# Two transformer layers on one core: the factor of the norm ahead of the gate product moved to the gate's output, norm weights multiplied ahead, the mixer's last tiles released one by one, the tail in halves

## The reference, cut to what matters

```python
mix = nsa_gmlp_mixer(rms_norm_2(h, norm_mix_pre), ...)      # ends in mixed @ w_out
h = h + rms_norm_2(mix, norm_mix_post)
gate, up = split(rms_norm_2(h, norm_ffn_pre) @ w_gate_up)   # 2816 columns each
ffn = (silu(gate) * up) @ w_down
h = h + rms_norm_2(ffn, norm_ffn_post)
# rms_norm_2(x, g) = x * rsqrt(mean(x * x) + 1e-6) * g
```

## Time and profile before

| | |
|---|---|
| runs | 1069.22, 1070.29, 1072.54 us (median 1070.29) |
| profiled execution | 1068.46 us |
| its span, first to last instruction | 1066.7 us |
| PE busy | 997.9 us (94%) |
| DVE, ACT, POOL busy | 407.6, 388.4, 391.0 us (36 to 38%) |
| mean granted PE clock | 0.985 of full |
| moved by DMA | 92.81 MB, mean 87 GB/s |

### The profile page before, as it was taken

How to read it: one execution, slowest core, us unless ns; L and a number is a source line. 1 busy time by engine, 2 the same in 40 slices (tenths; PEclk the granted TensorE clock), 3 DMA queues, 4 the chain that set the end, 5 groups by cost and what they waited for, 6 DMA issues and landing times.

```text
span 1066.7 us, 13142 instructions
## 1 busy us (share of the span) xinstructions
PE 997.9 (94%) x5055; PEld 816.8 (77%) x5055; DVE 407.6 (38%) x906; ACT 388.4 (36%) x720; POOL 391.0 (37%) x314
## 2 busy tenths in 40 slices
PE   6979999999998999989989899599999999999995
PEld 3867777767877887978878788488888888888884
DVE  3462631349655344437468642630000000122224
ACT  4232332343835233243555544432222322233332
POOL 4461422234221524123320015535444444454443
PEclk9989999999999999999999999799999999999998
DMA  6752121122115331052230002142323323232311
GB/s 225 201 176 48 48 72 40 42 78 65 40 41 198 119 119 61 23 181 77 75 104 2 1 1 82 41 136 79 104 94 91 106 81 117 80 119 79 119 40 79
DMA packets 68062, 92.81 MB, mean 87 GB/s; under 512 B 9740, under 2 KB 47153, under 8 KB 68000
## 3 DMA queue, kind: packets, MB, share of 16 engines
q1 hardware_dynamic: 68000, 91.97, 26.7%
HBM read 89.82 MB, written 6.85 MB: 91 GB/s over the span
## 4 chain that ended last, share of the span: by engine, by line
PE 82%; DVE 10%; issue 3%; ACT 2%; POOL 2%; DMA 1%; SPq 0%; DVEq 0%; ACTq 0%
PE psum L1010 62%; PE psum L1251 5%; PE psum L1211 4%; PE psum L1226 2%; POOL st L2099 1%; PE psum L1303 1%; PE psum L1084 1%; DVE prob L1837 1%; PE psum L1179 1%; PE psum L1279 1%; DVE sq L1739 1%; PE psum L1264 1%; DVE R L1867 1%; PE psum L1047 1%; PE psum L1293 1%
## 5 line engine op out<-in xcount | busy, mean ns | idle before, releaser
L2071 POOL TENSOR_TENSOR WR<-RAW,WR 128x512 fp32r<-128x512 f32 (+2 forms) x268 | 341.4, 1282 | 578.7 <-ACT WR L1390 578.7
L1010 PE MATMUL psum<-WR,XT 128*128 128x512 f32 (+2 forms) x2160 | 500.9, 387 | 5.8 <-DVE st L747 2.6
L1010 PEld LDWEIGHTS psum<-WR,XT 128*128 128x128 f32 x2160 | 390.3, 190 | 81.6 <-DVE st L747 3.4
L1390 ACT ACTIVATE WR<-RAW 128x512 fp32r<-128x512 f32 (+2 forms) x268 | 161.3, 615 | 263.3 <-PE psum L1010 251.0
L1010 PE MATMUL psum<-XT,WR 128*128 128x512 f32 x1056 | 241.8, 391 | 1.5 <-issue 1.5
L1010 PEld LDWEIGHTS psum<-XT,WR 128*128 128x128 f32 x1056 | 198.9, 189 | 43.1 <-issue 1.8
L1518 ACT ACTIVATE prob<-prob,st 128x512 f32<-128x512 f32 (+2 forms) x112 | 58.9, 547 | 160.4 <-DVE st L1837 146.7
L1692 DVE TENSOR_TENSOR actT<-psum,gated 128x512 f32<-128x512 f32 x22 | 14.2, 686 | 203.3 <-ACT gated L1470 203.3
L1251 PE MATMUL psum<-ones_up,probT 128*128 128x128 f32 x536 | 77.2, 285 | 12.5 <-DVE R L1867 8.3
L1251 PEld LDWEIGHTS psum<-ones_up,probT 128*128 128x128 f32 x536 | 68.5, 196 | 21.1 <-issue 13.7
L2028 DVE TENSOR_TENSOR XT<-actT,XT 128x512 fp32r<-128x512 f32 x22 | 28.4, 1290 | 84.6 <-ACT XT L1575 84.6
(11 more groups left out here) (210 smaller groups left out, 753.2 us busy)
## 6 DMA issues: line engine op xcount, KB each, us to landing
RAW<-in_w_gate_up_dram SPq DMA_DIRECT2D x44, 512.0 KB, 4.5
RAW<-in_w_in_dram SPq DMA_DIRECT2D x16, 1024.0 KB, 5.3
RAW<-in_w_down_dram SPq DMA_DIRECT2D x11, 1024.0 KB, 4.9
RAW<-in_w_out_dram SPq DMA_DIRECT2D x8, 1024.0 KB, 5.1
RAW<-in_w_in_dram SPq DMA_DIRECT2D x12, 512.0 KB, 4.5
rep_scratch<-rows_scratch SPq DMA_DIRECT2D x12, 320.0 KB, 7.2
R<-in_x_dram SPq DMA_DIRECT2D x4, 512.0 KB, 5.6
x_again<-in_x_dram SPq DMA_DIRECT2D x1, 2048.0 KB, 7.8
```

The costliest lines, as they stand in the source:

```text
L1010: last = pe.matmul(outp, stationary(x), moving(y), start=start and n == 0, stop=stop and n == 2)
L1390: act.activation(WR[:, s % RING, 0, 0:w], RAW[:, g % 2, q, 0:w], ACT.Copy).then_inc(w_hi, 1)
L2071: pool.tensor_tensor(WR[:, s % RING, 1, 0:w], RAW[:, g % 2, q, 0:w], WR[:, s % RING, 0, 0:w].bitcast(F32), ALU.subtract).then_inc(w_lo, 1)
```

## The change

- **The factor r1 and the weights.** With y the mixer's product, h = x + r1·y·g1. The new kernel does not form h before the gate product. During `out2` chunk 0 DVE makes XG = x·g0 (`xg`) and GG = g0·g1 (`gains`); `sqa` and `yg` make YG = y·g0·g1; `gx` makes YG·r1 + XG = h·g0 in one instruction per half, which is transposed.
- **The factor r2** of the norm ahead of the gate product is left out of the product's input. h itself (`res`, two DVE instructions of 128x1024 per tile) and its squares (`sq gu`) are made during gate chunk 0; r2 (`rr_x`) is then written to DRAM as a row of 512 values and read back broadcast to all partitions (`r_bc`, SP, `spread_r`). Every gate output is multiplied by it on DVE ahead of silu; the up output is not, and since the norm at the end takes out a factor of each token, only its epsilon is changed (`eps_x`).
- **Tiles released one by one.** The last k-step of `out2` is split into steps by tile (`mq`), with transposes of `xt gu` between them; the second half of y is copied out of its bank by ACT (`ycopy`), and the gate product waits for that (`y_copied`). The splits of gate slots 0 to 2 move from `out2` into this stretch.
- **Chunk 0 is evacuated later**, after k-step 3 of chunk 1.
- **The tail by halves.** Each tile's last down products go half by half; squares, the product with the gain (`yf`), the residual and the store (256 KB) are done for each half, all on DVE; POOL keeps the power.

The diff, cut to its core:

```diff
@@ make_timeline, out_product
-                if (phase, c, n) == ("out2", 1, KD - 1):
-                    tl.append(("mm", phase, c, n))
+                if (phase, c) == ("out2", 1) and n >= 4:
+                    tl.extend([("mm", phase, c, n)] if n < KD - 1 else [])
                 elif c or n >= begun:
                     mm(phase, c, n)
+                if phase == "out2" and c == 0 and n >= 4:
+                    tl.append(("xg", n - 4))
...
             if phase == "out2" and c == 0:
+                tl.append(("gains",))
                 tl.extend(("sqa", t) for t in range(NT))
@@ make_timeline, behind out2
-    for steps in (mix[0], post[0], mix[1], post[1], sq_gu[0], mix[2], post[2], sq_gu[1], mix[3], post[3], gx_gu[0][:1], gx_gu[1][:1], sq_gu[2]):
-        tl.extend(steps)
...
+    def finish(t):
+        return [("sq", "mix", t), ("ms", "mix", t), ("yg", t)]
+    row = [("mm", "out2", 1, KD - 1)] + [("mq", "out2", 1, KD - 1, t) for t in range(1, NT)]
+    tl.extend([row[0]] + finish(0))
+    tl.extend([row[1], ("gx", "gu", 0, 0)] + finish(1))
+    tl.extend([row[2], ("gx", "gu", 1, 0)] + finish(2) + [("xt", "gu", 0, 0), ("ycopy", 0)])
+    tl.extend([row[3], ("gx", "gu", 2, 0)] + finish(3) + [("gx", "gu", 3, 0), ("xt", "gu", 1, 0), ("xt", "gu", 2, 0)])
+    tl.extend([("split", first["gu", 0]), ("ycopy", 1), ("xt", "gu", 3, 0), ("ycopy", 2), ("ycopy", 3)])
+    tl.extend(("split", first["gu", 0] + j) for j in (1, 2))
+    tl.append(("split", first["gu", 0] + 3))
+    tl.append(("gx", "gu", 0, 1))
...
+            if c == 0 and 2 < k < 7:
+                tl.extend([("res", k - 3), ("sq", "gu", k - 3)])
+            if c == 0 and k == 6:
+                tl.append(("ms", "gu"))
+            if c == 1 and k == 3:
+                tl.append(("ev", "gu", 0))
+        if c:
+            tl.append(("ev", "gu", c))
...
+    for t in range(NT):
+        tl.extend([("sq", "ffn", t), ("yf", t, 0), ("ms", "ffn", t), ("yf", t, 1), ("post", "ffn", t)])
@@ SP
+            def spread_r():
+                sp.wait_ge(r_ready, nth["ms", "gu"] + 1)
+                sp.wait_ge(gx_done, nth["gx", "gu", 3, 1] + 1)
+                    sp.dma_start(r_d.rearrange("o (t p) -> p (o t)", p=P), rr_x).then_inc(r_stored, 16)
+                sp.wait_ge(r_stored, 16)
+                sp.dma_start(r_bc[:, :], r_d.broadcast_to([P, SEQ])).then_inc(rbc_done, 16)
...
-                index["gu", 2, 0]: [lambda: load_gain(1, "norm_ffn_post_2", (post_dve, NT))],
+                index["gu", 2, 0]: [spread_r, lambda: load_gain(1, "norm_ffn_post_2", (res_done, NT))],
...
+                for hf in range(2):
+                    cols = slice(512 * hf, 512 * hf + 512)
+                    sp.wait_ge(post_dve, 2 * t + hf + 1)
+                    sp.dma_start(out_v[:, t, cols], R2[:, t, cols]).then_inc(s_out, 16)
@@ PE
-                            order = [(kt, hf, t) for t in range(NT) for kt in tiles for hf in range(2)]
+                            order = [(kt, hf, t) for t in range(NT) for hf in range(2) for kt in tiles]
...
-                            pe.wait_ge(post_dve, NT)
+                            pe.wait_ge(y_copied, NT)
@@ ACT
+                elif what == "ycopy":
+                    act.wait_ge(yg_done, t + 1)
+                    act.activation(R1[:, t, 512:D], MM[t], ACT.Copy).then_inc(y_copied, 1)
...
-                            act.activation(gated[:, m, :], SET[ch % 2][m], ACT.Silu).then_inc(gs_done, 1)
+                            act.wait_ge(gate_scaled, 2 * ch + m + 1)
+                            act.activation(gated[:, m, :], gated[:, m, :], ACT.Silu).then_inc(gs_done, 1)
@@ DVE
+                        ins = dve.scalar_tensor_tensor(out=YG[:, t, cols], in0=YG[:, t, cols], scalar=rr[:, t:t + 1],
+                                                       in1=XG[:, t, cols], op0=ALU.mult, op1=ALU.add)
...
+                        dve.scalar_tensor_tensor(out=ss[:, t:t + 1], in0=ss[:, t:t + 1], scalar=floor, in1=ss_a[:, t:t + 1],
+                                                 op0=ALU.add, op1=ALU.add).then_inc(ms_ready, 1)
...
+                    dve.tensor_tensor(XG[:, t, :], R2[:, t, :], gain[0][:, :], ALU.mult).then_inc(xg_done, 1)
+                    dve.tensor_tensor(GG[:, :], gain[0][:, :], gain[1][:, :], ALU.mult).then_inc(gains_done, 1)
+                    dve.tensor_tensor(YG[:, t, 512:D], MM[t], GG[:, 512:D], ALU.mult).then_inc(yg_done, 1)
...
+                elif what == "res":
+                    dve.wait_ge(y_copied, t + 1)
+                    link(dve.tensor_tensor(R1[:, t, :], R1[:, t, :], gain[1][:, :], ALU.mult))
+                    dve.scalar_tensor_tensor(out=R2[:, t, :], in0=R1[:, t, :], scalar=rr[:, t:t + 1], in1=R2[:, t, :],
+                                             op0=ALU.mult, op1=ALU.add).then_inc(res_done, 1)
...
+                    last = dve.tensor_tensor(R1[:, t, cols], SET[hf][t], gain[1][:, cols], ALU.mult)
...
+                        dve.wait_ge(w_used, first[phase, ch] + KD)
+                        if ch == 0:
+                            dve.wait_ge(rbc_done, 16)
+                        for m in range(2):
+                            dve.tensor_tensor(gated[:, m, :], SET[ch % 2][m], r_bc[:, :], ALU.mult).then_inc(gate_scaled, 1)
...
+                    for hf in range(2):
+                        cols = slice(512 * hf, 512 * hf + 512)
+                        dve.scalar_tensor_tensor(out=R2[:, t, cols], in0=R1[:, t, cols], scalar=rr[:, t:t + 1], in1=R2[:, t, cols],
+                                                 op0=ALU.mult, op1=ALU.add).then_inc(post_dve, 1)
@@ POOL
-                if what == "post":
-                    pool.tensor_tensor(R2[:, t, cols], R2[:, t, cols], R1[:, t, cols], ALU.add).then_inc(post_pool, 1)
```

More of the change, by code:

```diff
@@ L575, in hybrid_two_block_kernel @@
         hot_r = sem("cmp_hots_copied")
+        gains_done = sem("gains_multiplied")
+        yga_done = sem("first_half_times_gains")
+        yg_done = sem("second_half_times_gains")
+        y_copied = sem("second_half_copied")
+        xg_done = sem("rows_times_pre_gain")
+        res_done = sem("residual_done")
+        r_stored = sem("r_row_stored")
+        rbc_done = sem("r_row_landed")
+        gate_scaled = sem("ffn_gate_scaled")
+        ffn_sq = sem("ffn_squares_summed")
         post_dve = sem("post_by_dve")
-        post_scaled = sem("post_scaled")
-        post_pool = sem("post_by_pool")
         xt_in = sem("xt_transposed")
@@ L961, in load_gmlp @@
                 bcast(ln_b[:, :], a["gmlp_ln_b_2"], 512).then_inc(s_gm_in, 16)
+            def spread_r():
+                sp.wait_ge(r_ready, nth["ms", "gu"] + 1)
+                sp.wait_ge(gx_done, nth["gx", "gu", 3, 1] + 1)
+                with nc.allow_non_contiguous_dma(reason="one row of 512 words, once"):
+                    sp.dma_start(r_d.rearrange("o (t p) -> p (o t)", p=P), rr_x).then_inc(r_stored, 16)
+                sp.wait_ge(r_stored, 16)
+                sp.dma_start(r_bc[:, :], r_d.broadcast_to([P, SEQ])).then_inc(rbc_done, 16)
             def load_gain(n, name, pre):
@@ L1085, in _ @@
                     last.then_inc(xt_in, 1)
-                elif what == "mm":
-                    _, phase, ch, n = step
+                elif what in ("mm", "mq"):
+                    _, phase, ch, n = step[:4]
                     s = first[phase, ch] + n
@@ L1116, in _ @@
                                     last.then_inc(w_used, 1)
[L1117 removed]
+                            elif kt == ch:
                                 last.then_inc(down_rows, 1)
@@ L1123, in _ @@
                     k = k_tile(phase, n)
-                    pe.wait_ge(w_lo, s + 1)
-                    if ch == 0 and n % 4 == 0:
+                    tiles = range(NT)
+                    if what == "mq":
+                        tiles = [step[4]]
+                    elif ("mq", phase, ch, n, 1) in nth:
+                        tiles = [0]
+                    if what == "mm":
+                        pe.wait_ge(w_lo, s + 1)
+                    if ch == 0 and n % 4 == 0 and what == "mm":
                         wait_rows(pe, phase, 1 if phase == "in1" else halves(phase)[n // 4], xt_lo)
@@ L1135, in _ @@
                     prev = ("ev", phase, ch - 1) if ch else {"in2": ("ev", "out1", 1)}.get(phase)
-                    for t in range(NT):
+                    for t in tiles:
                         if n == 0 and prev and phase != "gu":
@@ L1156, in _ @@
                                 last.then_inc(bank_full, 1)
-                    last.then_inc(w_used, 1)
+                    if NT - 1 in tiles:
+                        last.then_inc(w_used, 1)
                 elif what == "qt":
@@ L1427, in _ @@
                         act.wait_ge(tr_in, seen["tr"])
-                    act.activation(squares[:, t, :], R1[:, t, 0:512], ACT.Square, accum_out=ss_a[:, t:t + 1]).then_inc(sqa_done, 1)
```

(5 more changed lines are left out.)

139 lines of the change are left out of this document (70 added, 69 removed).

## The result

The changed kernel takes 1060.47 us (median of four, 1059.54 to 1061.53) against 1070.67 for the kernel before in the same comparison: ratio 0.9902, 95% interval 0.9888 to 0.9915. That is 10.2 us, inside the range (1052.5 to 1062) and faster, as forecast, but 3.4 us less than the 13.6 of my sum.

What follows compares the result with a forecast made beforehand. PE, busy for 94% of the span, bounds the kernel; only its standstills or slow clock can be won. -9.6 + 0 + 0.4 - 3.8 - 0.6 = -13.6 us gives 1056.7 from the median; forecast 1056.5, range 1052.5 to 1062.

Steps and rivals of the forecast that it cites:

- The norm: Mixer's closing norm, ahead of the gate product: first gate matmul at about 683.6 instead of 693.20, gain 9.6 us (8.6 to 9.9).
- The clock: PE's pause before the first gate matmul: slow-clock cost kept as before, 0 (bounds: gain 1.4, loss 0.6).
- What is made ahead: XG and gains, new on DVE, 6.3 us in all, fit its idle time before the norm: cost 0.
- res and the weight splits: Gate chunk 0: each res 3.85 us with one split added, split 11 done T+31.8 (T: first gate matmul), slack 0.6, cost 0.
- the 4.3: Sign of a wrong forecast in gate chunk 0: a res that takes over 4.3 us.
- The row of r2: r2 to DRAM and back: store T+30.6 to 34, weight group landed T+40.5, slack 3.5 us, cost 0; T is first gate matmul.
- my signs of being wrong: PE gap at gate slot 8 to 11 or 16, SP queue standing over 7 us, res over 4.3, or transposes waiting for gx.
- my third rival: The row of r2 is late, each us past the slack of 3.5 a stall: up to 1062; chance 0.10.
- The later chunks: Each later gate chunk gets two more PSUM-sourced DVE products, 22 in all, 14 us of DVE: cost 0.
- The first down product: It needs banks of the last gate chunk, whose DVE products end about 939.1 instead of 938.2: +0.4 us (0 to +1.0).
- The tail: After the last matmul: half-tile work on DVE gains 3.8 us (3.0 to 4.4), the half-sized last store 0.6 (0 to 0.8).
- the rivals: For the range: norm's remains hold weight splits (0.22, 1058 to 1060) and r2's row late (0.10, up to 1062).

Runs made afterwards that it cites:

- experiment 6: The changed kernel with the splits of gate slots 0 to 2 put back where the kernel before had them; 1060.7 us, ratio 0.9896.
- experiment 3: The changed kernel plus 12 matmuls that nothing reads, six ahead of the first halves' last transposes, six ahead of the first gate matmul; 1057.92 us.
- Experiments 1: The changed kernel with r2 stored as 128 pieces of 16 bytes and read by DVE with a stride in the gate scaling; 1056.96 us, ratio 0.9877.
- experiment 2: The changed kernel with SP's weight group of slots 16 to 19 ahead of the wait for the r2 store; 1058.18 us, ratio 0.9883.
- 7: The changed kernel with r2 stored in 16-byte pieces and one strided DVE copy into token order, scalings without stride; 1057.16 us, ratio 0.9865.
- experiment 9: Kernel 8 with a finer wait at the first down product: gate banks free after scaling, only up banks wait for the whole evacuation; 1054.2 us, ratio 0.9835.
- 4: The changed kernel again, unedited; 1060.04 us, ratio 0.9909.
- 8: The changed kernel with the edits of 7 and experiment 3, and ycopy 2 ahead of ACT's part of tile 3's transposes; 1052.84 us, ratio 0.9826.
- 10: The kernel of experiment 9 with 13 idle matmuls ahead of the very first transposes; 1054.5 us, ratio 0.9840.
- 5: The kernel before with only the tail of the change; 1066.12 us, ratio 0.9950.

## Why the prediction was right, and where its sum was off

- **The norm.** -9.6 forecast, -10.4 measured; from tile 0's squares to the first gate matmul I had 12.25 us and it is 11.43. The last wait is `ycopy`, the pauses are 1.4 and 1.8, transposes and gx lie at most 0.4 us from the forecast time, on the early side. The splits moved into it cost nothing (experiment 6).
- **The clock.** I took 0, with a gain of 1.4 and a loss of 0.6 as bounds; it is a loss of 1.45 from the first k-step to the second, outside them. That the clock falls was right; the size failed at both ends. It fell at 683.0, 4.0 us after the product's last matmul, where my two rows had 4.9 and 5.3. And I kept the cost of before: there it was back at 696.0, 2.8 us after the first gate matmul, here at 689.8, 5.9 us after it, so that all 12 matmuls ran slow. Why it came back later is not shown. A fill keeps it up (experiment 3).
- **What is made ahead** (XG, GG): 0, as forecast; DVE has 12.0 us idle before tile 0's statistics, as before.
- **res and the weight splits**: 0, right, but priced too high, and that the times agree in the changed kernel is luck. There the last res ends 27.6 us after the first gate matmul (27.7 forecast), the power 30.3 (30.5), split 11 31.5 (31.8). But I had counted at the fast clock, and the slow first k-step is 2.8 us longer (5.96 against 3.2 to the second). Experiment 3, with the clock up, has 24.8, 27.6 and 28.8: all about 3 us earlier than forecast. The four res take 13.0 us together, not 4 x 3.85 = 15.4. Three of their eight instructions had a split of POOL beside them and took 2.2 to 2.3 us, the others 1.2 to 1.3. Both of the third res had one:

```profile
704.43 2.32 DVE L1741 TENSOR_TENSOR R<-R,gain 128x1024 f32<-128x1024 f32 x1
...
706.78 2.19 DVE L1742 SCALAR_TENSOR_TENSOR R<-R,st,R 128x1024 f32<-128x1024 f32 x1
```

  With 4.5 this res is over the 4.3 that I had named as a sign of being wrong, and it cost nothing, because the slack at slot 11 was about 3 us and not 0.6.
- **The row of r2.** This step failed: "Store T+30.6 to 34", from a word-wise load of 3.3 us. The store took 9.73, so the group went out at T+40.9 and landed at T+49.2, where I had 35.5 and 40.5, and the slack of 3.5 became a wait of 2.55. Two more of my signs of being wrong stand there: an SP queue that stood 10.6 us between r2's power and the weight group, and a PE gap at slot 16. The store was 6.3 us over its price and the group 2.7; that only 2.55 reached PE is owed to the res, which let the store go 3 us earlier, by the fast clock, than I had it. The mechanism was my third rival, at 0.10, whose reason ("a store of 512 single words, each a packet, has no row here") should have opened the bound upward in the sum too. The load had moved 1024 words in its 3.3 us; a load from DRAM into SBUF is no price for a store the other way. Experiments 1, 2 and 7 show it.
- **The later chunks**: 0, right: from the second gate k-step to the first down product it is 238.3 us before (697.71 to 936.05) and 241.2 after (689.83 to 931.05), 2.55 of it the wait before chunk 2 and 0.3 beside it (last point). The first down product +0.4, measured 0.39 to 0.43 (120.23 and 120.27 against 119.84) and taken away by experiment 9's edit.
- **The tail**: -3.8 and -0.6 forecast, -4.1 and -0.6 measured in the trace (7.65 to 3.57 up to DVE's end, 3.15 to 2.51 behind it), and -5.1 (3.4 to 7.2) alone in the kernel before. That of the store's 2.6 us half would stay was a guess without a row; it came out.
- Sum of the differences from the norm on: -10.4 + 1.45 + 3.3 - 4.7 = -10.35, and up to tile 0's squares the execution took 1.06 longer. Of the 3.3, the wait is 2.55 and the down product 0.4. The other 0.3 goes with a recorded wait of PE: after, 1 to 4 and 6, each with one, all lose 0.28 to 0.36 beside it, 7, 8 and 10, with none, nothing. So the idle time that the profile records is that much shorter than what a wait costs.

The time lies 4 us above the forecast of 1056.5. It is inside the range because the range's upper end was taken from the rivals.

## What to carry to other kernels

When a value must cross partitions through DRAM, lay it out so that each partition writes its words as one piece and put the order right later, once, on chip. When SP has to wait for a landing, count everything queued behind the wait, and price a DMA only from a row of the same direction and piece size. When a forecast time comes out, check that the terms under it did too: here two shifts of about 3 us cancelled. A stall removed from PE is worth its length only if PE doesn't come out of it at the low clock: count the matmuls behind a pause at the clock that the pause leaves.

## What the runs showed of the hardware that was not expected

- Storing 512 words of 4 bytes to DRAM took 9.6 to 10.8 us to landing in five runs; as 128 pieces of 16 bytes the same 2 KB took 2.0 to 2.1 in four. Weights issued beside the slow store took 11.9 us (experiment 2).
- A DVE product with a PSUM source took 1.06 us for 128x512 with its SBUF operand read at a stride of four words (and all operands cut into four pieces), 0.69 without; a strided copy of the same row from SBUF to SBUF takes 0.61.
- The start of this kernel comes in two forms. In the profiles of 5 and 8 the 8 matmuls of the first tables take 2.96 us and the first weight product starts at 19.7 us, in all others 5.71 and 23.3 to 24.3. That this is PE's clock is read from the length and from experiment 10, where the granted clock is 0.50 beside 5.71; the profiles of the kernels before and after show 1.00 beside the same 5.71, so there the row and the lengths disagree. Those two profiled executions, 1060.19 and 1049.47 us, are the fastest of their kernel, 5.9 and 3.4 under its median. Experiment 5 has the start of the kernel before, so the same can be expected there and may be what widens the intervals; no profile of the kernel before shows it. What decides it is open.
- On transposes and the clock the rows point both ways. It stayed at 0.50 through 687 to 693 us of the kernel before and fell among transposes in experiment 10, while two groups of six matmuls of 128x512 in the pauses kept it at 1.00. But in the starts of 5 and 8 PE had run nothing but transposes, the first eight slowly (2.21 us), when its tables ran at the fast length: there the clock came up among them. No rule follows from these runs.
